# A first expert's tokens gathered apart from its group, and fewer warming matmuls ahead of the experts

## The chip, the cores and the metric

One core of a Trainium2 chip (trn2). The metric is device time in microseconds of one execution; the kernel before took 934.81 us (median of 3 runs, 934.11 to 937.46).

## The reference, cut to what matters

```python
for l in range(DEPTH):                       # DEPTH = 2
    h = rmsnorm(x, norm1_g[l]);  x = x + token_mixers(h, ...)      # four mixers, merged, projected
    h = rmsnorm(x, norm2_g[l]);  x = x + hierarchical_moe(h, ...)
return rmsnorm(x, norm_f_g)

def hierarchical_moe(h, ...):                # h: 256 tokens x 1024
    group = top1(softmax(h @ w_rg + b_rg))                         # 4 groups
    top2 experts of that group's 8, weights = p_group * softmax(their logits)
    # 32 experts, each: (silu(h @ w_g[e]) * (h @ w_u[e]) * comb[:, e]) @ w_d[e]
    # w_g[e], w_u[e]: 1024 x 256; w_d[e]: 256 x 1024, all float32
```

## The kernel before, in words

Each of the two layers is a mixer stage and an expert stage. The orders below are written out by hand, one program per engine, joined by semaphores (`then_inc`, `wait_ge`; `L(s, v)` is the value v counted within the layer).

**From mixer to experts.** VectorE adds the last projection to `x` (L1793, semaphore `x_mid`, once for each half of the tokens). TensorE transposes `x` (L711, 16 matmuls), multiplies it by the router's weights `wr` (L719, 16 matmuls whose moving operand is 36 columns wide), and then `keep_warm(11, 7)` issues 11 matmuls on constants whose result nobody reads (L403). Another `keep_warm(4, 7)` stands ahead of the transposes. VectorE meanwhile works out top-1 group and top-2 experts (L1813 to L1854, `member_ok`); TensorE ranks the tokens of each expert (L726 to L729), and VectorE makes `pick`, a 0/1 matrix of tokens by slots (L1861): a group of the kernel is GE = 4 experts, each has SLOTS = 32 slots, so that one group is 128 slots. There are 8 groups in a layer.

**A group's tokens.** `gather` (L740) multiplies `wide` (the normalised tokens, 128x128 blocks, as stationary operand) by `pick` (128 slots, as moving operand): 8 blocks of channels by 2 halves of the tokens, 16 matmuls in fp32, for which the profile shows 32 weight loads and 32 matmuls. Its two PSUM banks are scaled into `hG[g % 2]` by VectorE, 512 columns each (L1893, `gath_out`). `hG[0]` lies over `qkr`, `hG[1]` over `yy`.

**An expert.** `gate_up` (L753) multiplies the expert's 32 slots by its gate and up weights, 32 matmuls (64 in the profile), and signals `gu_mm`; ScalarE takes the SiLU (L1212), VectorE the product (L1904), TensorE transposes it (L759), `down` (L767) multiplies it by the down weights and signals `down_mm`. TensorE runs two experts ahead: `gate_up` of e + 2 stands before `down` of e. When e is a group's first expert, the gather of the next group stands before that.

**The weights.** SyncE's queue brings them, 1 MB a transfer, gate and up of an expert one behind the other (L340), down apart (L344). There is room for RP = 6 pairs and RD = 7 downs. `FIRST_LOADS` fills all of it; then every further transfer waits for its place:

```python
for kind, e in NEXT_LOADS:               # pairs 6, 7, 8, then pair 9, down 7, pair 10, down 8, ...
    if kind == "gu":
        sp.wait_ge(*L(gu_mm, e - RP + 1)); load_gate_up(sp, e, l)
    else:
        sp.wait_ge(*L(down_mm, e - RD + 1)); load_down(sp, e, l)
```

So pair 6 is asked for when `gate_up` of expert 0 is done, pair 7 after that of expert 1, pair 8 after that of expert 2. Behind the last expert's transfers the first units of the next layer's mixer weights follow on the same queue.

Of the kernel before, what the change touches and what calls it, by code (L numbers as in the profile page):

```python
# [17 lines left out]
P = 128  # L18
# [61 lines left out]
for _e in range(RD, NE):  # L80
# [16 lines left out]
    rank_mm=1, passes_ok=1,  # L97
    pick_ok=GROUPS, wpick_ok=GROUPS, gath_mm=2 * GROUPS, gath_out=2 * GROUPS, scat_T=GROUPS, scatT_out=GROUPS,
    gu_mm=NE, silu_out=NE, hid_out=NE, hid_T=NE, hidT_out=NE, down_mm=NE, y_act=NE, y_dve=NE,
# [3 lines left out]
def build(nc, x_in, positions, norm1_g, w_in, sgu_ln_g, sgu_ln_b, w_spatial, b_spatial, conv_w, w_branch,  # L103
          w_out, norm2_g, w_rg, b_rg, w_re, b_re, w_eg, w_eu, w_ed, norm_f_g, out):
    ctx = ExitStack()
    with ctx:
# [97 lines left out]
        def sem(name):  # L204
            return ctx.enter_context(nc.semaphore(name))
# [34 lines left out]
            sem("gexp"), sem("emax"), sem("eexp"), sem("member_ok"), sem("rank_mm"))  # L240
        passes_ok = sem("passes_ok")
        wide_mm = sem("wide_mm")
# [157 lines left out]
        def keep_warm(k, bank_no):  # L400

            for _ in range(k):
                nc.tensor.matmul(ps[:, bank_no, 0:P], ones[:], ident[:], start=True, stop=True,  # L403
                                 skip_group_check=True)
# [4 lines left out]
        def bank(b, n=1):  # L409
            return ps[:, b, :] if n == 1 else ps[:, b:b + n, :]  # L410


        with nc.Block() as whole:

            @whole.tensor
            def _(pe):
# [7 lines left out]
                for l in range(DEPTH):  # L424
# [281 lines left out]
                    pe.wait_ge(layer_loaded, 16 * 5 * (l + 1))  # L706
                    keep_warm(4, 7)
                    for t in range(TT):
# [6 lines left out]
                    for t in range(TT):  # L715
# [5 lines left out]
                        ins.then_inc(route_mm, 1)  # L721
                    keep_warm(11, 7)

# [9 lines left out]

                    def gather(g, dst_done):

                        for b in range(2):
                            for c in range(4):
                                cc = 4 * b + c
                                for t in range(TT):
                                    ins = mm(ps[:, b, P * c:P * c + P], wide[:, t, P * cc:P * cc + P],  # L740
                                             pick[:, t, :], start=(t == 0), stop=(t == TT - 1),
                                             skip_group_check=True)
                            if dst_done is gath_mm or b == 1:
                                ins.then_inc(dst_done, 1)
# [31 lines left out]
                    def gather_group(g):  # L776
                        pe.wait_ge(*L(pick_ok, g + 1))
                        if g == 0:
                            pe.wait_ge(*L(xn_act, 1))
                            pe.wait_ge(*L(xn_dve, 1))  # L780
                        if g >= 3:
                            pe.wait_ge(*L(x_add, 4 * (g - 2)))
                        gather(g, gath_mm)

                    def gate_up_expert(e):
                        pe.wait_ge(*gu_loads(e, l))
                        if e % GE == 0:
                            pe.wait_ge(*L(gath_out, 2 * (e // GE) + 1))
                        gate_up(pair_slot(e, l), hG[e // GE % 2], e % GE, 2 + e % 2, gu_mm,
                                L(gath_out, 2 * (e // GE) + 2) if e % GE == 0 else None)  # L790

# [24 lines left out]
                    def hid_expert(e):  # L816
# [3 lines left out]
                        hid_transposes(e % 2, hid_T)  # L820

                    gather_group(0)
                    gate_up_expert(0)
                    gate_up_expert(1)
# [624 lines left out]
            def _(dve):  # L1449
# [3 lines left out]
                def link(ins):  # L1453

                    n[0] += 1
                    ins.then_inc(dve_c, 1)
                    dve.wait_ge(dve_c, n[0])
# [37 lines left out]
                for l in range(DEPTH):  # L1495
# [388 lines left out]

                    link(V.tensor_reduce(cnts, ps[:, 2, 64:96], AX.X, ALU.max))
                    beyond = prod32.rearrange("p t g e -> p (t g e)")[:, 0:MAXPASS]
                    link(V.tensor_tensor(beyond, cnts.broadcast_to([P, MAXPASS]), limits[:], ALU.is_gt))
                    link(V.tensor_reduce(cnts, beyond, AX.X, ALU.add))
                    V.tensor_copy(npass[:], cnts[0:1, :]).then_inc(passes_ok, 1)

                    def gather_evac(dst, b):

                        return V.tensor_tensor(dst[:, 4 * b:4 * b + 4, :], bank(b).rearrange("p (c s) -> p c s", c=4),  # L1893
                                               small[:, PG2 + 4 * b:PG2 + 4 * b + 4]
                                               .rearrange("p (c o) -> p c o", o=1).broadcast_to([P, 4, P]), ALU.mult)

                    def gather_out(g):
                        for b in range(2):
                            dve.wait_ge(*L(gath_mm, 2 * g + b + 1))
                            gather_evac(hG[g % 2], b).then_inc(gath_out, 1)  # L1900

# [6 lines left out]
                    def hidden_expert(e):  # L1908
                        dve.wait_ge(*L(silu_out, e + 1))
                        hidden(e % 2, 2 + e % 2).then_inc(hid_out, 1)  # L1910

                    def add_group(g, banks):
                        for k in range(4):
# [3 lines left out]
                            V.tensor_tensor(xs, xs, bank(banks[k]), ALU.add).then_inc(x_add, 1)  # L1917

                    gather_out(0)
                    pick_group(1)  # L1920
                    hidden_expert(0)
                    hidden_expert(1)
# [83 lines left out]
```

## Time and profile before

| | |
|---|---|
| median of 3 runs | 934.81 us (934.11 to 937.46) |
| the profiled execution | 935.73 us, its span 934.0 us |
| TensorE busy / its weight loads | 843.5 us (90%) / 670.8 us (72%) |
| VectorE / ScalarE / GpSimd busy | 534.1 us (57%) / 389.5 us (42%) / 114.6 us (12%) |
| mean DMA rate | 301 GB/s; 281.45 MB moved |
| mean granted clock of TensorE | 0.958 of full speed |

Times in the rows are microseconds from the start of the span. PE is TensorE's matmuls, PEld its weight loads (they overlap), DVE VectorE, ACT ScalarE, POOL GpSimd, SPq SyncE's DMA issues. In brackets stands the idle time before a piece and what ended it. A busy TensorE says little by itself, since many of its matmuls are warming or wait on their weight loads; the order of events around one release says more.

### The profile page before, as it was taken

The page shows a single profiled execution, that of the slowest core. Times are in us where ns is not written, and L with a number is a line of the kernel's source. Part 1 is how long each engine was busy: PE and PEld are TensorE (multiplying, and loading weights), DVE is VectorE, ACT ScalarE, POOL GpSimd, SP SyncE. Part 2 cuts the span into 40 slices and gives each one's busy share as a digit, 9 for nine tenths or more (in the row PEclk, how much of TensorE's full clock was granted, in tenths as well). Part 3 has the DMA queues.
Part 4 walks back from the last instruction along what each step waited for, and adds up shares of the span by engine and source line. Part 5 has one row for each costly group of instructions (what it writes and reads, how often), then busy time and mean ns, then how long its engine had stood idle before and what let it go on. Part 6 is the DMA issues. An engine that isn't in the chain of part 4 may idle for free.

```text
span 934.0 us, 19930 instructions
## 1 busy us (share of the span) xinstructions
PE 843.5 (90%) x8583; PEld 670.8 (72%) x8583; DVE 534.1 (57%) x1072; ACT 389.5 (42%) x676; POOL 114.6 (12%) x168
## 2 busy tenths in 40 slices
PE   7999899999999988867899997999999999777775
PEld 6997778887987756654579976888789767554543
DVE  5677668667555533423476676885746555333424
ACT  5547667645412211111265567674544222211114
POOL 6700101211000000000055001022200000000000
PEclk9999999999999989988999999999999999988978
DMA  9965444473899999999996453456578999999993
GB/s 271 361 241 178 138 136 144 172 299 151 354 378 418 418 419 420 420 420 420 399 360 236 137 183 108 157 182 223 226 269 335 419 419 420 420 419 420 420 420 125
DMA packets 63516, 281.45 MB, mean 301 GB/s; under 512 B 5024, under 2 KB 7152, under 8 KB 38848
## 3 DMA queue, kind: packets, MB, share of 16 engines
q1 hardware_dynamic: 62144, 278.18, 76.6%
q0 software_dynamic: 800, 1.40, 0.9%
q8 instruction: 70, 1.15, 0.5%
q10 hardware_dynamic: 480, 0.54, 0.2%
q14 instruction: 22, 0.18, 0.1%
HBM read 279.06 MB, written 1.05 MB: 300 GB/s over the span
## 4 chain that ended last, share of the span: by engine, by line
PE 57%; DMA 18%; DVE 7%; ACT 7%; issue 5%; SPq 4%; POOL 2%; POOLq 0%; DVEq 0%; ACTq 0%
DMA ring<-in_w_exp_up 15%; PE ps L436 9%; PE ps L438 9%; PE ps L437 9%; PE ps L753 9%; PE ps L740 4%; PE ps L813 4%; PE ps L767 4%; DMA late<-in_w_exp_up 3%; SPq L340 3%; DVE split_lo L1506 2%; PE ps L403 2%; ACT split_hi L998 1%; POOL wide L1399 1%; PE ps L759 1%
## 5 line engine op out<-in xcount | busy, mean ns | idle before, releaser
L1506 DVE TENSOR_TENSOR split_lo<-ring,split_hi 128x1024 fp32r<-128x1024 f32 (+1 forms) x143 | 195.8, 1410 | 46.1 <-ACT split_hi L998 41.7
L436 PE MATMUL ps<-split_hi,hT_hi 128*128 128x512 f32 (+2 forms) x416 | 162.8, 391 | 15.7 <-DVE split_lo L1506 12.6
L438 PE MATMUL ps<-split_hi,hT_lo 128*128 128x512 f32 (+2 forms) x416 | 159.4, 383 | 0.0
L437 PE MATMUL ps<-split_lo,hT_hi 128*128 128x512 f32 (+2 forms) x416 | 159.4, 383 | 0.0
L998 ACT ACTIVATE split_hi<-ring 128x1024 fp32r<-128x1024 f32 (+1 forms) x140 | 141.4, 1053 | 27.3 <-PE ps L438 24.7
L1904 DVE TENSOR_TENSOR br<-br,ps 32x64 f32<-32x64 f32 x256 | 54.9, 214 | 162.9 <-ACT br L1212 160.3
L1212 ACT ACTIVATE br<-ps 128x64 f32<-128x64 f32 x64 | 14.3, 224 | 266.3 <-PE ps L753 266.3
L436 PEld LDWEIGHTS ps<-split_hi,hT_hi 128*128 128x128 f32 x416 | 79.4, 191 | 35.7 <-DVE split_lo L1506 17.8
L438 PEld LDWEIGHTS ps<-split_hi,hT_lo 128*128 128x128 f32 x416 | 79.3, 191 | 14.8
L437 PEld LDWEIGHTS ps<-split_lo,hT_hi 128*128 128x128 f32 x416 | 79.4, 191 | 13.4
L753 PE MATMUL ps<-ring,yy 128*32 128x128 f32 x1664 | 60.8, 306 | 24.2 <-DMA ring<-in_w_exp_up 24.1
L753 PEld LDWEIGHTS ps<-ring,yy 128*32 128x32 f32 x1664 | 52.1, 123 | 34.7 <-DMA ring<-in_w_exp_up 27.7
L753 PE MATMUL ps<-ring,qkr 128*32 128x128 f32 x1792 | 60.7, 293 | 17.9 <-DMA ring<-in_w_exp_up 17.2
L753 PEld LDWEIGHTS ps<-ring,qkr 128*32 128x32 f32 x1792 | 52.8, 118 | 25.6 <-DMA ring<-in_w_exp_up 22.8
L1416 POOL TENSOR_TENSOR idx<-idx,wt 128x128 f32<-128x128 f32 x32 | 12.1, 399 | 411.2 <-PE ps L773 327.6
L740 PEld LDWEIGHTS ps<-idx,wide 128*128 128x128 f32 x512 | 58.4, 192 | 5.0 <-issue 4.9
L740 PE MATMUL ps<-idx,wide 128*128 128x128 f32 x512 | 61.2, 278 | 0.0
L1399 POOL TENSOR_TENSOR wide<-wide,qkr 128x1024 f32<-128x1024 f32 x10 | 33.1, 3310 | 183.2 <-DVE qkr L1682 183.2
L1917 DVE TENSOR_TENSOR x<-x,ps 128x512 f32<-128x512 f32 x64 | 44.0, 688 | 16.0 <-PE ps L813 16.0
L767 PE MATMUL ps<-late,br 128*32 128x256 f32 x704 | 49.4, 399 | 1.3 <-DMA late<-in_w_exp_down 1.1
L436 PE MATMUL ps<-hT_hi,split_hi 128*128 128x256 f32 x160 | 45.6, 285 | 0.0
L437 PE MATMUL ps<-hT_lo,split_hi 128*128 128x256 f32 x160 | 45.3, 283 | 0.0
(264 smaller groups left out, 1274.9 us busy)
## 6 DMA issues: line engine op xcount, KB each, us to landing
ring<-in_w_exp_gate SPq DMA_DIRECT2D x54, 1024.0 KB, 24.6
ring<-in_w_exp_up SPq DMA_DIRECT2D x54, 1024.0 KB, 26.0
ring<-in_w_in SPq DMA_DIRECT2D x52, 1024.0 KB, 6.5
late<-in_w_exp_down SPq DMA_DIRECT2D x44, 1024.0 KB, 26.8
ring<-in_w_exp_down SPq DMA_DIRECT2D x20, 1024.0 KB, 26.7
late<-in_w_exp_gate SPq DMA_DIRECT2D x10, 1024.0 KB, 25.2
late<-in_w_exp_up SPq DMA_DIRECT2D x10, 1024.0 KB, 26.4
ring<-in_w_branch SPq DMA_DIRECT2D x8, 1024.0 KB, 4.9
```

Source lines behind the costliest of these rows:

```text
L436: mm(dst, st[0], mv[0], start=start, stop=False, skip_group_check=True)
L437: mm(dst, st[0], mv[1], start=False, stop=False, skip_group_check=True)
L438: return mm(dst, st[1], mv[0], start=False, stop=stop, skip_group_check=True)
L740: ins = mm(ps[:, b, P * c:P * c + P], wide[:, t, P * cc:P * cc + P], pick[:, t, :], start=(t == 0), stop=(t == TT - 1), skip_group_check=True)
L753: ins = mm(ps[32 * j:32 * j + 32, b, 0:P], hg[:, c, SLOTS * i:SLOTS * i + SLOTS], w[:, :, c, 64 * j:64 * j + 64], start=(c == 0), stop=(c ...
L767: ins = mm(ps[32 * q:32 * q + 32, b, 0:256], hidT[:, par, k, :], w[:, k, 256 * q:256 * q + 256], start=(k == 0), stop=(k == 1))
L813: mm(bank(banks[k]), scatT[:, t, :], y_slots[g % 2][:, 512 * hf:512 * hf + 512], start=True, stop=True).then_inc(scat_mm, 1)
L998: A(half_view(split_hi[:, v % SPLITS, :], v), raw_half(v, l), ACT.Copy).then_inc(hi_done, 1)
L1399: nc.gpsimd.tensor_tensor(m, m, sig[:], ALU.add).then_inc(gate_sum, 1)
L1506: V.tensor_tensor(half_view(split_lo[:, v % SPLITS, :], v), raw_half(v, l), half_view(split_hi[:, v % SPLITS, :], v).bitcast(F32), ALU.sub ...
L1904: ins = V.tensor_tensor(hid[:, par, 64 * j:64 * j + 64], silu[32 * j:32 * j + 32, par, :], ps[32 * j:32 * j + 32, b, 64:128], ALU.mult)
L1917: V.tensor_tensor(xs, xs, bank(banks[k]), ALU.add).then_inc(x_add, 1)
```

## The change

The first expert of group 0 gets a gather of its own. `gather_lead` runs the same 16 matmuls with only its 32 slots as moving operand, into PSUM bank 4; VectorE scales the result in one instruction of 256 columns, and `gate_up` of expert 0 waits for that (`lead_out`). The gather of group 0 follows behind it with the other 96 slots, its two evacuations 384 columns each, and `gate_up` of expert 1 waits for these. On VectorE the evacuation of the lead stands ahead of the last three steps of the pass count, for whose end GpSimd waits (`passes_ok`), and expert 0's product ahead of the gather's evacuations and of `pick` for group 1. `keep_warm(4, 7)` is gone and `keep_warm(11, 7)` is `keep_warm(8, 7)`. All of it holds for both layers.

```diff
-                    keep_warm(4, 7)
                     for t in range(TT):
                         pe.wait_ge(*L(x_mid, t + 1))
...
-                    keep_warm(11, 7)
+                    keep_warm(8, 7)
...
-                    def gather(g, dst_done):
+                    def gather(g, dst_done, s0=0):
...
-                                    ins = mm(ps[:, b, P * c:P * c + P], wide[:, t, P * cc:P * cc + P],
-                                             pick[:, t, :], start=(t == 0), stop=(t == TT - 1),
+                                    ins = mm(ps[:, b, P * c + s0:P * c + P], wide[:, t, P * cc:P * cc + P],
+                                             pick[:, t, s0:], start=(t == 0), stop=(t == TT - 1),
...
-                        gather(g, gath_mm)
+                        gather(g, gath_mm, SLOTS if g == 0 else 0)
+
+                    def gather_lead():
+                        pe.wait_ge(*L(pick_ok, 1))
+                        pe.wait_ge(*L(xn_act, 1))
+                        pe.wait_ge(*L(xn_dve, 1))
+                        for c in range(C):
+                            for t in range(TT):
+                                ins = mm(ps[:, 4, SLOTS * c:SLOTS * c + SLOTS], wide[:, t, P * c:P * c + P],
+                                         pick[:, t, 0:SLOTS], start=(t == 0), stop=(t == TT - 1), skip_group_check=True)
+                        ins.then_inc(lead_mm, 1)
...
                         pe.wait_ge(*gu_loads(e, l))
-                        if e % GE == 0:
+                        first_of = 1 if e < GE else 0
+                        if e == 0:
+                            pe.wait_ge(*L(lead_out, 1))
+                        elif e % GE == first_of:
                             pe.wait_ge(*L(gath_out, 2 * (e // GE) + 1))
...
+                    gather_lead()
+                    gate_up_expert(0)
                     gather_group(0)
-                    gate_up_expert(0)
                     gate_up_expert(1)
...
                     link(V.tensor_reduce(cnts, ps[:, 2, 64:96], AX.X, ALU.max))
+                    dve.wait_ge(*L(lead_mm, 1))
+                    V.tensor_tensor(hG[0][:, :, 0:SLOTS], ps[:, 4, 0:C * SLOTS].rearrange("p (c s) -> p c s", c=C),
+                                    small[:, PG2:PG2 + C].rearrange("p (c o) -> p c o", o=1).broadcast_to([P, C, SLOTS]),
+                                    ALU.mult).then_inc(lead_out, 1)
...
+                    hidden_expert(0)
                     gather_out(0)
                     pick_group(1)
-                    hidden_expert(0)
                     hidden_expert(1)
```

TensorE's order, layer 0, from the last projection (L438) to the gather of group 1 (L740, moving operand in columns behind the partitions; L753 is gate and up, 32 matmuls an expert). Before:

```order
L438 MATMUL ps<-split_hi,hT_lo 128x512
L403 MATMUL ps<-ident,ones 128x128 x4
L711 MATMUL ps<-ident,x 128x128 x16
L719 MATMUL ps<-wr,late 128x36 x16
L403 MATMUL ps<-ident,ones 128x128 x11
L726 MATMUL ps<-br,incl_T 128x64
L727 MATMUL ps<-br,ones 128x64
L729 MATMUL ps<-br,ones 128x32
L403 MATMUL ps<-ident,ones 128x128 x5
L740 MATMUL ps<-idx,wide 128x128 x16
L753 MATMUL ps<-ring,qkr 32x128 x64
L759 MATMUL ps<-ident,br 128x32 x2
```

The same place in the changed kernel (its lines are numbered a few lower or higher):

```order
L718 MATMUL ps<-wr,late 128x36 x16
L403 MATMUL ps<-ident,ones 128x128 x8
L725 MATMUL ps<-br,incl_T 128x64
L726 MATMUL ps<-br,ones 128x64
L728 MATMUL ps<-br,ones 128x32
L403 MATMUL ps<-ident,ones 128x128 x5
L787 MATMUL ps<-idx,wide 128x32 x16
L752 MATMUL ps<-ring,qkr 32x128 x32
L739 MATMUL ps<-idx,wide 128x96 x16
L752 MATMUL ps<-ring,qkr 32x128 x32
L758 MATMUL ps<-ident,br 128x32 x2
```

Sixteen matmuls on the same 16 blocks of `wide` are added ahead of expert 0, and the group's own gather, 96 columns wide, now stands between expert 0 and expert 1.

VectorE's order in the changed kernel, layer 0, from the expert weights `wt` on (L1897 is the lead's evacuation, L1907 the gather's, L1919 an expert's product, L1871 `pick`):

```order
L1891 TENSOR_TENSOR wt<-br 128x64
L1895 TENSOR_REDUCE br<-ps 128x1
L1897 TENSOR_TENSOR qkr<-ps,small_all 128x8x32
L1901 TENSOR_TENSOR br<-br,limits 128x8
L1902 TENSOR_REDUCE br<-br 128x1
L1903 CAST npass<-br 1x1
L1919 TENSOR_TENSOR br<-br,ps 32x64 x4
L1907 TENSOR_TENSOR qkr<-ps,small_all 128x4x96 x2
L1871 TENSOR_TENSOR idx<-rankm,slot_no 128x2x128
L1919 TENSOR_TENSOR br<-br,ps 32x64 x4
```

Before, the two evacuations of 512 columns and `pick` for group 1 stood right behind `npass`, ahead of both products.

## Rows read from the trace of the kernel before

**Rows 1.** The page: the DMA rate (GB/s) in 40 equal slices of the span.
```profile
GB/s 271 361 241 178 138 136 144 172 299 151 354 378 418 418 419 420 420 420 420 399 360 236 137 183 108 157 182 223 226 269 335 419 419 420 420 419 420 420 420 125
```

**Rows 2.** The chain that ended last, in order of time: start us, us, what.
```profile
446.36 3.50 PE ps L753 x64
...
875.74 26.32 DMA ring<-in_w_exp_up
902.11 3.64 PE ps L753 x64
```

**Rows 3.** Stretches around the first release of a pair in each layer; columns in the first line.
```profile
core 0: us, PE busy (x) PEld busy (x) DVE busy (x) ACT busy (x) POOL busy (x), PEclk, DMA share, GB/s
260.00:263.50 3.50, 3.50 (x96) 3.34 (x98) 1.26 (x3) 0.22 (x1) 0.00 (x0) 1.00 0.65 269
263.50:267.00 3.50, 3.50 (x71) 3.26 (x63) 1.71 (x8) 0.45 (x2) 0.00 (x0) 1.00 0.82 272
716.00:719.50 3.50, 3.50 (x111) 3.34 (x114) 1.51 (x5) 0.22 (x1) 0.00 (x0) 1.00 0.62 255
719.50:723.00 3.50, 3.07 (x52) 2.57 (x41) 1.23 (x6) 0.45 (x2) 0.00 (x0) 1.00 0.97 318
```

**Rows 4.** SyncE's DMA issues in order of time, layer 0: start us, us, line, transfer.
```profile
263.24 0.33 SPq L340 DMA_DIRECT2D ring<-in_w_exp_gate  x1
...
264.98 0.33 SPq L340 DMA_DIRECT2D ring<-in_w_exp_gate  x1
...
270.99 0.33 SPq L340 DMA_DIRECT2D ring<-in_w_exp_gate  x1
...
274.08 0.33 SPq L340 DMA_DIRECT2D ring<-in_w_exp_gate  x1
```

**Rows 5.** The same, layer 1.
```profile
718.72 0.33 SPq L340 DMA_DIRECT2D ring<-in_w_exp_gate  x1
...
721.13 0.33 SPq L340 DMA_DIRECT2D ring<-in_w_exp_gate  x1
...
727.16 0.33 SPq L340 DMA_DIRECT2D ring<-in_w_exp_gate  x1
```

**Rows 6.** Timeline, layer 0, from the last residual add to expert 1.
```profile
244.31 2.65 DVE L1793 TENSOR_TENSOR x<-x,ps 128x512 f32<-128x512 f32 x4 [7.20 <-PE ps L438]
...
246.25 1.78 PEld L711 LDWEIGHTS ps<-ident,x 128*128 128x128 f32 x16
...
248.00 3.66 PEld L719 LDWEIGHTS ps<-wr,late 128*128 128x128 f32 x32
...
251.57 4.17 PEld L403 LDWEIGHTS ps<-ident,ones 128*128 128x128 f32 x22
...
254.91 0.22 DVE L1854 TENSOR_TENSOR br<-br 128x64 f32<-128x64 f32 x1
255.66 0.30 PEld L726 LDWEIGHTS ps<-br,incl_T 128*128 128x128 f32 x2
...
257.45 3.65 PEld L740 LDWEIGHTS ps<-idx,wide 128*128 128x128 f32 x32
...
261.22 3.43 PEld L753 LDWEIGHTS ps<-ring,qkr 128*32 128x32 f32 x128
...
261.33 0.69 DVE L1893 TENSOR_TENSOR qkr<-ps,small_all 128x512 f32<-128x512 f32 x1 [1.09 <-PE ps L740]
261.94 0.42 DVE L1861 TENSOR_TENSOR idx<-rankm,slot_no 128x256 f32<-128x256 f32 x1
```

**Rows 7.** Timeline, layer 1, warming and the start of the ranking.
```profile
707.56 2.54 PEld L403 LDWEIGHTS ps<-ident,ones 128*128 128x128 f32 x22
...
710.87 0.22 DVE L1854 TENSOR_TENSOR br<-br 128x64 f32<-128x64 f32 x1
711.15 0.30 PEld L726 LDWEIGHTS ps<-br,incl_T 128*128 128x128 f32 x2 [1.05 <-DVE br L1854]
```

**Rows 8.** A stretch of layer 0 with the granted clock (PEclk), same columns as rows 3.
```profile
251.50:255.00 3.50, 3.50 (x19) 3.50 (x19) 2.78 (x19) 2.98 (x5) 0.00 (x0) 0.51 1.02 431
```

More of the change, by code:

```diff
@@ L97 @@
     rank_mm=1, passes_ok=1,
-    pick_ok=GROUPS, wpick_ok=GROUPS, gath_mm=2 * GROUPS, gath_out=2 * GROUPS, scat_T=GROUPS, scatT_out=GROUPS,
+    lead_mm=1, lead_out=1, pick_ok=GROUPS, wpick_ok=GROUPS, gath_mm=2 * GROUPS, gath_out=2 * GROUPS, scat_T=GROUPS, scatT_out=GROUPS,
     gu_mm=NE, silu_out=NE, hid_out=NE, hid_T=NE, hidT_out=NE, down_mm=NE, y_act=NE, y_dve=NE,
@@ L240, in build @@
             sem("gexp"), sem("emax"), sem("eexp"), sem("member_ok"), sem("rank_mm"))
-        passes_ok = sem("passes_ok")
+        passes_ok, lead_mm, lead_out = sem("passes_ok"), sem("lead_mm"), sem("lead_out")
         wide_mm = sem("wide_mm")
@@ L777, in gather_group @@
                         pe.wait_ge(*L(pick_ok, g + 1))
-                        if g == 0:
-                            pe.wait_ge(*L(xn_act, 1))
-                            pe.wait_ge(*L(xn_dve, 1))
                         if g >= 3:
                             pe.wait_ge(*L(x_add, 4 * (g - 2)))
-                        gather(g, gath_mm)
+                        gather(g, gath_mm, SLOTS if g == 0 else 0)
[8 more added lines that the diff above has]
+                        ins.then_inc(lead_mm, 1)
                     def gate_up_expert(e):
                         pe.wait_ge(*gu_loads(e, l))
-                        if e % GE == 0:
+                        first_of = 1 if e < GE else 0
+                        if e == 0:
+                            pe.wait_ge(*L(lead_out, 1))
+                        elif e % GE == first_of:
                             pe.wait_ge(*L(gath_out, 2 * (e // GE) + 1))
                         gate_up(pair_slot(e, l), hG[e // GE % 2], e % GE, 2 + e % 2, gu_mm,
-                                L(gath_out, 2 * (e // GE) + 2) if e % GE == 0 else None)
+                                L(gath_out, 2 * (e // GE) + 2) if e and e % GE == first_of else None)
                     def down_expert(e):
@@ L1889, in _, with gather_evac @@
                     V.tensor_copy(npass[:], cnts[0:1, :]).then_inc(passes_ok, 1)
-                    def gather_evac(dst, b):
-                        return V.tensor_tensor(dst[:, 4 * b:4 * b + 4, :], bank(b).rearrange("p (c s) -> p c s", c=4),
+                    def gather_evac(dst, b, s0=0):
+                        return V.tensor_tensor(dst[:, 4 * b:4 * b + 4, s0:],
+                                               bank(b).rearrange("p (c s) -> p c s", c=4)[:, :, s0:],
                                                small[:, PG2 + 4 * b:PG2 + 4 * b + 4]
-                                               .rearrange("p (c o) -> p c o", o=1).broadcast_to([P, 4, P]), ALU.mult)
+                                               .rearrange("p (c o) -> p c o", o=1).broadcast_to([P, 4, P - s0]), ALU.mult)
                     def gather_out(g):
@@ L1899, in gather_out @@
                             dve.wait_ge(*L(gath_mm, 2 * g + b + 1))
-                            gather_evac(hG[g % 2], b).then_inc(gath_out, 1)
+                            gather_evac(hG[g % 2], b, SLOTS if g == 0 else 0).then_inc(gath_out, 1)
                     def hidden(par, b):
```

## The prediction

> **What bounds the kernel now.** I read the DMA rate over the span first. In each expert stage it stands at 418 to 420 GB/s slice after slice [rows 1]: there the kernel takes weights as fast as they come. The chain that ended last confirms it: in both layers it ends on a weight transfer of over 26 us and then on the `gate_up` that had waited for it [rows 2]. So a microsecond in which the DMA engines stand idle early in an expert stage is missing at its end, and a microsecond that TensorE gains or loses there counts only if it moves a transfer. The question is then when the queue runs dry, and for that I read short stretches and SyncE's issues.
>
> `FIRST_LOADS` asks for all that there is room for, and the next issue is that of pair 6 at 263.24 [rows 4], when expert 0's `gate_up` has freed a place. In the 3.5 us up to 263.5 the mean rate is 269 GB/s and in the 3.5 us behind it 272 [rows 3]. Against the full 420 that is a flow that ends at 260 + 3.5 x 269/420 = 262.24 and one that begins at 267 - 3.5 x 272/420 = 264.73: 2.5 us idle, and 1.49 us from the issue to the flow. In layer 1 the same working gives 718.13 and 720.35 [rows 3], 2.2 us idle, and 1.63 us behind the issue at 718.72 [rows 5]. These two holes, 4.7 us together, are all that an earlier expert 0 could win.
>
> **The lead gather.** The group's gather takes 3.65 us of weight loads for 32 of them, and 3.77 us pass from its start at 257.45 to that of `gate_up` at 261.22 [rows 6]. What does a moving operand of 32 columns save? The router's matmuls have the same 128-column stationary operand and only 36 moving columns, and their 32 loads take 3.66 us [rows 6], the same. So the stationary side sets the pace and the narrower operand saves nothing: I take 3.77 us. The other bound is the `gate_up` form, whose 128 loads are 32 columns wide and take 3.43 us, 27 ns each [rows 6]: 32 x 27 ns = 0.9 us if the loads cost nothing at all. The router's row is by far the nearer, so the sum goes by it. TensorE: Matmul & The Clock Gate, a page of the Trainium skill, has in its section on the back-to-back issue gap a form by which the spacing is N/2.4 + 2.5 ns with a floor of about 25 ns, which would make the lead some 0.8 us (an estimate by that page); with that the sum would be the third rival's below. The trace disagrees here (3.66 us at 36 moving columns, 3.65 at 128).
>
> **What stands between it and expert 0.** Before, `gate_up` began as the gather ended, for the first half had been evacuated meanwhile, and the second evacuation (261.33, 0.69 us) was needed only at half way [rows 6]. Now TensorE must wait for the lead's evacuation: 0.11 us from the matmul's end to VectorE (261.22 to 261.33), 0.42 us for 256 columns (the `pick` of that size), 0.06 us back to TensorE (VectorE's last routing step ends at 710.87 + 0.22 = 711.09, and TensorE begins at 711.15 [rows 6, 7]). That is a bubble of 0.59 us. VectorE's chain of small steps is over long before; the three `npass` steps behind the wait delay GpSimd's first product by some 3 us, which nobody needs before the transposes two experts later: nothing.
>
> **Warming.** `keep_warm(4)` ends at 246.25, where the transposes begin; the residual adds end at 244.31 + 2.65 = 246.96 and the second half of the transposes needs them [rows 6], at 246.25 + 0.89 = 247.14 before and 247.02 now. Of the 1.0 us taken out, 0.12 us is won. `keep_warm(11)` ran until 255.66 in layer 0 though `member_ok` was there at 254.91 + 0.22 = 255.13 [rows 6], since the granted clock was 0.51, the 1.2 GHz level, in that stretch [rows 8]. With three matmuls fewer and 0.12 us won ahead of it, the ranking starts when `member_ok` comes, at 255.13 - 0.12 + 0.06 = 255.07, 0.59 us earlier. In layer 1 the warming was over early and TensorE waited 1.05 us for VectorE [rows 7]: only the 0.12 us there. Savings: 0.59 and 0.12 us.
>
> **Expert 0** then ends at +0.59 - 0.59 = 0 in layer 0 and at +0.59 - 0.12 = +0.47 us in layer 1. It is not earlier. **Experts 1 and 2** come a whole gather later, for the other 96 slots need all 16 stationary blocks once more: another 3.77 us. Their evacuations (each under 0.69 us) are hidden, the first under the gather's second half, the second under the first half of `gate_up` (3.7/4 = 0.9 us); expert 0's product, now ahead of them, is done before the first. So the releases of pairs 7 and 8 come 3.77 us later in layer 0 and 3.77 + 0.47 = 4.24 us later in layer 1.
>
> **What of it reaches the DMA queue.** A pair is 2.1 MB, 4.99 us at 420 GB/s; pair 8 would begin to flow two pairs behind the restart. Layer 0: before at 264.73 + 9.98 = 274.71; now its issue is at 270.99 + 3.77 = 274.76 [rows 4] and its flow 1.49 us later, 276.25: **1.5 us lost**. Pair 7's own lateness (268.75 + 1.49 against 269.72, half a microsecond) lies within that, since the latest release decides. Layer 1: before at 720.35 + 9.98 = 730.33; now 727.16 + 4.24 + 1.63 = 733.03 [rows 5]: **2.7 us lost**. Pair 9 is asked for 3.1 us behind pair 8 (270.99 and 274.08 [rows 4]), while pair 8's 5 us still flow, and what follows has more in hand. What of the 1.5 us from issue to flow still counts when the queue is not quite empty, no row shows; from below it is nothing, which gives 0.1 and 1.1 us, from above the whole of it, which gives 1.5 and 2.7. The queue would have only about half a microsecond left at those issues, so I take the upper value.
>
> **Sum:** +4.2 us. The profiled execution (935.73 us) is 0.9 us above the median of 934.81; against the median that makes **939.0 us**, 0.45% slower.
>
> **Rivals.** *The clock falls in the lead.* In layer 0 it fell to the 1.2 GHz level at 251.5, right behind the 3.66 us of narrow router matmuls, and came back at 255 [rows 6, 8]; in layer 1, same instructions, it did not. The lead gather is another narrow stretch of the same length with an idle bubble behind it. If the clock falls there, it is expert 0 and the second gather that run slowly: the same 22 warming loads took 4.17 us in layer 0 and 2.54 in layer 1, so 1.6 us a fall [rows 6, 7], all of it on the release of pair 8. In one layer that gives 940.6, in both 942.2. The same page of the Trainium skill says that the clock gate falls when TensorE is little used, and the trace bears it out once in two such places; so about one in three for each lead, a third of the chance altogether.
> *The latency from issue to flow is hidden* by what is left in the queue: +1.2 us, 936.0, to some 938 if half of it is.
> *Not slower: narrow matmuls are short after all.* With the lead at 0.9 us, expert 0 ends 2.9 and 2.4 us earlier, and both holes close. Pair 8 then decides: its release shifts by 3.77 - 2.87 + 0.59 less the savings, +0.9 and +1.37 us, its flow begins at 273.4 instead of 274.7 and at 730.2 instead of 730.3: -1.5 us, 933.3. If 96 columns are in proportion cheaper too (2.8 us), it is -3.4 us, 931.4. The two layers break even, by the same working, at a lead of some 1.6 us. Against it stands the router's row.
> *The change doesn't reach its place:* it would need a wait that holds the lead, but `pick` and the normalised tokens are both there when the gather starts today.
>
> **Chances.** Forecast 0.40, clock 0.33, hidden latency 0.15, not slower 0.06, something unseen 0.06 (either side). A measurement of this kernel can tell about 0.5% (4.7 us, so 930.1 to 939.5) from no change. The forecast lies just inside, with its own spread of half a microsecond a layer about two thirds of it; with the latency case, the not-slower case and a little of the clock case that makes 0.52 for no change, 0.46 for slower, 0.02 for faster. The range runs from the hidden latency, 936.0, to a fall in both layers, 942.3.
>
> **What would show it.** Right: in the changed kernel, 32 weight loads of 3.6 us for the lead and again for the 96 columns; TensorE idle 0.6 us between lead and expert 0; pair 6 issued no earlier behind the ranking than before, pairs 7 and 8 about 4 us later; a DMA hole ahead of pair 6 as before and a second one of a microsecond ahead of pair 8; everything from there to the end of the layer shifted by 1.5 to 2.7 us. Wrong: a lead well under 3 us, or a queue that never runs dry a second time.

## The result and the profile after

The changed kernel took 949.02 us (median of 4 runs, 944.12 to 950.75) against 934.66 us before: ratio 1.014, 95% interval 1.0119 to 1.0161. I had forecast 939.0 us in a range of 936.0 to 942.3. The sign is right and the size is not: 14.4 us are lost instead of 4.2. The profiled execution took 950.75 us, its span 948.8 us, 14.8 longer than before.

The page of the changed kernel, the DMA rate over 40 slices [rows 1]:

```profile
GB/s 271 364 226 175 133 134 176 136 347 128 379 317 422 418 420 420 420 420 420 395 350 205 146 180 91 152 191 232 204 252 284 377 419 419 420 419 420 420 421 143
```

The two expert stages still run at 418 to 422 GB/s once they run; it is the slices just ahead (317; 284 and 377) that got thin. The chain of the changed kernel still ends on weights and on the `gate_up` that waited for them [rows 2], so the loss was suffered where the queue was dry:

```profile
423.77 27.58 DMA ring<-in_w_exp_up
451.40 3.64 PE ps L752 x64
...
891.03 26.55 DMA ring<-in_w_exp_up
917.62 3.31 PE ps L752 x64
```

The timeline of the changed kernel around the lead in layer 0 (L787 is the lead, L752 `gate_up`, L739 the other 96 slots, L1897 the lead's evacuation), beside [rows 6]:

```profile
257.43 3.65 PEld L787 LDWEIGHTS ps<-idx,wide 128*128 128x128 f32 x32
...
261.30 0.42 DVE L1897 TENSOR_TENSOR qkr<-ps,small_all 128x256 f32<-128x256 f32 x1 [2.75 <-PE ps L787]
...
261.84 2.51 PEld L752 LDWEIGHTS ps<-ring,qkr 128*32 128x32 f32 x64 [0.76 <-issue]
...
264.74 4.27 PEld L739 LDWEIGHTS ps<-idx,wide 128*128 128x128 f32 x32 [0.38 <-issue]
...
269.11 1.69 PEld L752 LDWEIGHTS ps<-ring,qkr 128*32 128x32 f32 x64
```

The lead's 32 weight loads take 3.65 us with 32 moving columns, as those of the full gather did. TensorE then stands 0.76 us. But expert 0's loads take 2.51 us where expert 1's take 1.69, and the second gather's 4.27 where the lead's took 3.65: the granted clock had fallen. Layer 1, the same place:

```profile
719.27 1.54 PEld L403 LDWEIGHTS ps<-ident,ones 128*128 128x128 f32 x10
720.69 6.95 PEld L787 LDWEIGHTS ps<-idx,wide 128*128 128x128 f32 x32
728.42 3.22 PEld L752 LDWEIGHTS ps<-ring,qkr 128*32 128x32 f32 x64 [0.78 <-issue]
732.02 4.44 PEld L739 LDWEIGHTS ps<-idx,wide 128*128 128x128 f32 x32 [0.38 <-issue]
736.56 1.69 PEld L752 LDWEIGHTS ps<-ring,qkr 128*32 128x32 f32 x64
```

Here the lead itself took 6.95 us. The stretches of the changed kernel say why (columns as in [rows 3]: TensorE, its loads, VectorE, ScalarE, GpSimd, granted clock, DMA share, GB/s):

```profile
262.50:266.00 3.50, 3.50 (x57) 3.12 (x47) 0.85 (x4) 0.22 (x1) 0.57 (x2) 0.52 0.32 59
...
718.00:721.50 3.50, 2.89 (x20) 2.89 (x20) 2.28 (x13) 1.16 (x1) 0.00 (x0) 0.79 1.01 426
721.50:725.00 3.50, 3.50 (x18) 3.50 (x18) 0.01 (x1) 0.00 (x0) 0.00 (x0) 0.50 1.01 421
725.00:728.50 3.50, 2.82 (x18) 2.72 (x21) 0.58 (x3) 0.00 (x0) 0.00 (x0) 0.50 0.22 87
728.50:732.00 3.50, 3.50 (x64) 3.14 (x64) 0.21 (x2) 0.00 (x0) 0.76 (x2) 0.50 0.00 0
732.00:735.50 3.50, 3.50 (x28) 3.48 (x25) 1.42 (x5) 0.23 (x1) 0.00 (x0) 0.76 0.66 227
```

In layer 0 the clock is at the 1.2 GHz level from 262.7 to 266.1. In layer 1 it stays there from 720.1 to 733.7, 13.7 us, through the end of the warming, the lead, its bubble, expert 0 and the start of the second gather, with TensorE all but continuously busy. The DMA engines, which had been drained by 725.7, stand still until 733.6: eight microseconds where there had been two. SyncE's issues in layer 1 [rows 5]:

```profile
732.14 0.33 SPq L340 DMA_DIRECT2D ring<-in_w_exp_gate  x1
...
738.57 0.33 SPq L340 DMA_DIRECT2D ring<-in_w_exp_gate  x1
...
744.58 0.33 SPq L340 DMA_DIRECT2D ring<-in_w_exp_gate  x1
```

Counted from the issue of pair 5 at the mixer's end (701.65 before, 709.28 after), pairs 6, 7 and 8 are asked for at 22.9, 29.3 and 35.3 us instead of 17.1, 19.5 and 25.5.

**A measure for all runs.** For every profile I took the times of these issues from pair 5's on, and the DMA rate in 60 stretches of 1 us, from 4 us behind pair 5's issue on, summed as (420 - rate)/420: the DMA time that is missing in that part. The table stands behind the experiments.

### The profile page after: what moved, and what is told of

The parts are those of the page before. It is cut to its first block, busy times and chain, and to the rows that moved or that the text cites. A ratio compares the mean times of both kernels' runs of the same rounds, so it can differ in the third digit from the quotient of the medians.

```text
span 948.8 us, 20010 instructions
## 1 busy us (share of the span) xinstructions
PE 861.0 (91%) x8619; PEld 682.9 (72%) x8619; DVE 533.8 (56%) x1074; ACT 389.6 (41%) x676; POOL 114.5 (12%) x168
## 3 DMA queue, kind: packets, MB, share of 16 engines
HBM read 279.06 MB, written 1.05 MB: 295 GB/s over the span
## 4 chain that ended last, share of the span: by engine, by line
PE 59%; DMA 18%; DVE 7%; ACT 7%; issue 5%; SPq 2%; POOL 2%; DVEq 0%; POOLq 0%; ACTq 0%
DMA ring<-in_w_exp_up 14%; PE ps L436 10%; PE ps L752 9%; PE ps L438 9%; PE ps L437 9%; PE ps L739 5%; PE ps L766 4%; PE ps L822 4%; DMA late<-in_w_exp_up 3%; DVE split_lo L1516 2%; PE ps L403 2%; ACT split_hi L1008 1%; SPq L340 1%; POOL wide L1409 1%; PE ps L758 1%
## 5 line engine op out<-in xcount | busy, mean ns | idle before, releaser
L436 PE MATMUL ps<-split_hi,hT_hi 128*128 128x512 f32 (+2 forms) x416 | 162.9, 392 | 16.9 <-DVE split_lo L1516 13.7
L438 PE MATMUL ps<-split_hi,hT_lo 128*128 128x512 f32 (+2 forms) x416 | 159.4, 383 | 0.0
L1008 ACT ACTIVATE split_hi<-ring 128x1024 fp32r<-128x1024 f32 (+1 forms) x140 | 141.5, 1053 | 27.1 <-PE ps L438 25.3
L1919 DVE TENSOR_TENSOR br<-br,ps 32x64 f32<-32x64 f32 x256 | 54.9, 215 | 161.9 <-ACT br L1222 159.3
L438 PEld LDWEIGHTS ps<-split_hi,hT_lo 128*128 128x128 f32 x416 | 79.5, 191 | 14.8
L752 PE MATMUL ps<-ring,yy 128*32 128x128 f32 x1664 | 61.5, 309 | 24.5 <-DMA ring<-in_w_exp_up 24.5
L752 PEld LDWEIGHTS ps<-ring,yy 128*32 128x32 f32 x1664 | 52.6, 124 | 35.0 <-DMA ring<-in_w_exp_up 27.8
L752 PE MATMUL ps<-ring,qkr 128*32 128x128 f32 x1792 | 62.7, 298 | 13.1 <-DMA ring<-in_w_exp_up 11.7
L752 PEld LDWEIGHTS ps<-ring,qkr 128*32 128x32 f32 x1792 | 54.1, 119 | 21.2 <-DMA ring<-in_w_exp_up 16.0
L739 PEld LDWEIGHTS ps<-idx,wide 128*128 128x128 f32 x512 | 59.9, 196 | 6.3 <-issue 6.2
L739 PE MATMUL ps<-idx,wide 128*128 128x128 f32 (+1 forms) x512 | 63.1, 282 | 0.1
```

Of the source, the lines that this page charges most:

```text
L436: mm(dst, st[0], mv[0], start=start, stop=False, skip_group_check=True)
L438: return mm(dst, st[1], mv[0], start=False, stop=stop, skip_group_check=True)
L739: ins = mm(ps[:, b, P * c + s0:P * c + P], wide[:, t, P * cc:P * cc + P], pick[:, t, s0:], start=(t == 0), stop=(t == TT - 1), skip_group_ ...
L752: ins = mm(ps[32 * j:32 * j + 32, b, 0:P], hg[:, c, SLOTS * i:SLOTS * i + SLOTS], w[:, :, c, 64 * j:64 * j + 64], start=(c == 0), stop=(c ...
L1008: A(half_view(split_hi[:, v % SPLITS, :], v), raw_half(v, l), ACT.Copy).then_inc(hi_done, 1)
L1919: ins = V.tensor_tensor(hid[:, par, 64 * j:64 * j + 64], silu[32 * j:32 * j + 32, par, :], ps[32 * j:32 * j + 32, b, 64:128], ALU.mult)
```

## The experiments

Theory A, from the trace: the narrow lead drops the clock. Rival B: the missing warming does. Rival C: the clock hardly matters, and the extra gather costs the DMA queue much more than the 4.2 us that I worked out. The first four kernels cross the two parts: lead narrow or wide, warming cut or whole.

**e1, the changed kernel with both warming blocks back.**

```diff
+                    keep_warm(4, 7)
                     for t in range(TT):
...
-                    keep_warm(8, 7)
+                    keep_warm(11, 7)
```

> The changed kernel with both warming blocks as before (4 and 11 matmuls). Theory A (the narrow lead gather itself, 3.65 us of 32-column matmuls and a 0.6 us bubble, drops the granted clock in expert 0 and the second gather): the clock still falls there in most executions, 943 to 947 us. Rival B (the missing warming drops the clock): no fall in the lead, 939 to 940 us. Rival C (neither: the extra gather costs far more at the DMA queue than the 4.2 us I gave it): 947 to 950 us, with the clock full.

Measured: 941.99 us (936.68 to 945.52, 7 runs) against 934.36, ratio 1.0089 (1.0056 to 1.0122). In its profile the clock fell right behind the lead, in expert 0, in layer 0 (260.1 to 263.5), and not in layer 1. The median lies between A's range and B's, nearer to A's, and the clock still fell with all the warming back: B falls as the whole cause. Yet the warming is worth 5.5 to 6.7 us here: the kernel is 7.6 us slower than the one before, and the change 14.4 (13.1 when it was measured again, e10 below).

**e2, the kernel before with the cut warming and no lead.**

```diff
-                    keep_warm(4, 7)
...
-                    keep_warm(11, 7)
+                    keep_warm(8, 7)
```

> The kernel before with the two cuts in warming alone (no block of 4, 8 instead of 11), no lead gather. A: nothing to lose, ranking up to 0.6 us earlier, 934.0 to 934.8 us. B: the clock falls in the gather or in expert 0, 937 us or more. C: as A.

Measured: 936.71 us (934.13 to 938.16, 10 runs), ratio 1.0018 (1.0002 to 1.0034). What I had counted as a gain of 0.7 us is a loss of 1.7 us (0.2 to 3.2). The weight loads of its layer 1 show a part of it:

```profile
709.33 1.87 PEld L403 LDWEIGHTS ps<-ident,ones 128*128 128x128 f32 x16
712.91 0.30 PEld L725 LDWEIGHTS ps<-br,incl_T 128*128 128x128 f32 x2 [1.71 <-DVE br L1853]
...
713.58 2.10 PEld L403 LDWEIGHTS ps<-ident,ones 128*128 128x128 f32 x10
715.55 4.42 PEld L739 LDWEIGHTS ps<-idx,wide 128*128 128x128 f32 x32
```

TensorE idles 1.71 us behind the shorter warming, the clock falls at 713.7 and the full gather takes 4.42 us instead of 3.65. In the kernel before, the clock fell in layer 0 only, during the warming itself [rows 6, 8], where it cost half a microsecond. In layer 0 of e2 it did not fall here at all, and pair 8 is asked for 0.7 us earlier: there the saving came. So only a part of the loss is traced. The two layers together miss 0.6 us more DMA time than before; of the 2.4 us by which this profile's span is longer, 1.6 lie in the mixer of layer 1, which the edit does not touch.

**e3, the changed kernel with a wide lead.** Same order, waits and number of loads, but all 128 slots as moving operand, written into banks 0 and 1 instead of bank 4.

```diff
-                                ins = mm(ps[:, 4, SLOTS * c:SLOTS * c + SLOTS], wide[:, t, P * c:P * c + P],
-                                         pick[:, t, 0:SLOTS], start=(t == 0), stop=(t == TT - 1), skip_group_check=True)
+                                ins = mm(ps[:, c // 4, P * (c % 4):P * (c % 4) + P], wide[:, t, P * c:P * c + P],
+                                         pick[:, t, :], start=(t == 0), stop=(t == TT - 1), skip_group_check=True)
...
-                    V.tensor_tensor(hG[0][:, :, 0:SLOTS], ps[:, 4, 0:C * SLOTS].rearrange("p (c s) -> p c s", c=C),
+                    V.tensor_tensor(hG[0][:, :, 0:SLOTS], ps[:, 0:2, :].rearrange("p b (c s) -> p (b c) s", c=4)[:, :, 0:SLOTS],
```

> The changed kernel, but the lead gather takes all 128 slots as moving operand (into banks 0 and 1, of which only expert 0's 32 slots are evacuated): same 32 weight loads, same order, same waits, wide matmuls. A: the clock stays full through lead, expert 0 and second gather, 938.5 to 940 us; pairs 7 and 8 asked for 3.8 and 4.2 us later than before. B: as the changed kernel, 944 to 950 us. C: 947 to 950 us with the clock full.

Measured: 942.20 us (940.67 to 943.33, 4 runs), ratio 1.0086 (1.0064 to 1.0107). Four times as many moving columns in the lead make the kernel 5.3 to 6.5 us faster. C falls, and B as the whole cause. A's 940 us at most is missed by 2: the clock did not stay full, it fell behind the short warming, as B has it, and the lead's loads took 4.89 us. But it came back within the lead, and expert 0 and the second gather ran at full speed:

```profile
254.01 1.63 PEld L403 LDWEIGHTS ps<-ident,ones 128*128 128x128 f32 x10
255.52 4.89 PEld L787 LDWEIGHTS ps<-idx,wide 128*128 128x128 f32 x32
261.25 1.72 PEld L752 LDWEIGHTS ps<-ring,qkr 128*32 128x32 f32 x64 [0.84 <-issue]
263.17 3.65 PEld L739 LDWEIGHTS ps<-idx,wide 128*128 128x128 f32 x32 [0.20 <-issue]
```

**e4, the wide lead and both warming blocks** (the edits of e1 and e3 together).

> The wide lead and both warming blocks as before. A: 939.0 to 940.5 us (the bubble of 0.6 us without the 0.6 and 0.1 us saved). B: the same, since warming is there. C: 947 us or more.

Measured: 940.59 us (939.19 to 943.07, 4 runs), ratio 1.0072 (1.0045 to 1.0099). A holds. This is what the change costs when the clock falls neither in the lead nor behind it: its profile has falls in the warming alone, and 3.65 us of loads for the lead in both layers. The rest of the steps, in layer 1:

```profile
718.13 3.65 PEld L788 LDWEIGHTS ps<-idx,wide 128*128 128x128 f32 x32
722.63 1.72 PEld L753 LDWEIGHTS ps<-ring,qkr 128*32 128x32 f32 x64 [0.84 <-issue]
724.54 3.65 PEld L740 LDWEIGHTS ps<-idx,wide 128*128 128x128 f32 x32 [0.20 <-issue]
728.28 1.69 PEld L753 LDWEIGHTS ps<-ring,qkr 128*32 128x32 f32 x64
```

**e5, the second gather's time alone.** Sixteen wide matmuls on constants in the kernel before:

```diff
                     gate_up_expert(0)
+                    keep_warm(16, 7)
                     gate_up_expert(1)
```

> The kernel before with 16 wide matmuls on constants between expert 0 and expert 1: the second gather's TensorE time alone, no lead, no bubble, no cut in warming. If the loss of the wide lead with full warming (940.6 us against 934.4) is the later release of pairs 7 and 8, this gives releases of pairs 7 and 8 3.8 us later and a DMA hole ahead of pair 8 in each layer: +1.5 and +2.2 us, 937.5 to 938.5 us. If the bubble and the evacuation ahead of expert 0 are the larger part, 935 to 936 us. If something else of the change (order on VectorE, GpSimd's later start) carries it, 934.4 us.

Measured: 939.08 us (935.91 to 941.64, 10 runs) against 935.32, ratio 1.0034 (1.0016 to 1.0052), which is 3.2 us (1.5 to 4.9), and 3.8 by the medians. The first case holds. In layer 0 the filler takes the gather's 3.65 us and the issues follow it:

```profile
263.32 0.33 SPq L340 DMA_DIRECT2D ring<-in_w_exp_gate  x1
...
268.98 0.33 SPq L340 DMA_DIRECT2D ring<-in_w_exp_gate  x1
...
274.98 0.33 SPq L340 DMA_DIRECT2D ring<-in_w_exp_gate  x1
```

Pair 6 stands where it stood [rows 4], pairs 7 and 8 come 3.9 us later from pair 5's issue on.

**e6, the changed kernel with the 11 back, the 4 still out.**

```diff
-                    keep_warm(8, 7)
+                    keep_warm(11, 7)
```

> The changed kernel with 11 warming matmuls instead of 8; the block of 4 ahead of the transposes stays out. If the three matmuls taken from behind the router are what lets the clock fall into the narrow lead, this is as the changed kernel with both blocks back, 941 to 943 us. If the block of 4 does it, about 947 to 949 us. Both in equal parts: 944 to 946 us.

Measured: 943.40 us (936.06 to 949.49, 10 runs), ratio 1.0066 (1.0039 to 1.0094). Mostly the first case: the three matmuls behind the router carry most of what warming does here. The runs lie in groups, two at 936.1, seven from 941.5 to 944.1, one at 949.5. In its profile (943.36 us) the clock fell in both layers, in expert 0 for 3 us in layer 0, and in the lead for 7 us in layer 1.

**e7, another way at the same DMA hole.** The kernel before, but half a place given back in the middle of expert 0:

```diff
+                            if first and c == C // 2 - 1:
+                                ins.then_inc(gu_half, 1)
...
+                        if kind == "gu" and e == RP:
+                            sp.wait_ge(*L(gu_half, 1))
+                            load_half_pair(sp, e, l, 0)
+                            sp.wait_ge(*L(gu_mm, 1))
+                            load_half_pair(sp, e, l, 1)
```

> The kernel before, with the place of pair 0 given back in two halves: after the first four of eight channel blocks of expert 0's gate and up, SyncE asks for the first halves of pair 6's gate and up (0.5 MB each), after the last block for the second halves. It goes at the same DMA hole as the change, without a gather more. First issue 0.9 us earlier, DMA hole 0.9 us shorter in each layer: 932.5 us against 934.4, ratio 0.998. If halves of 0.5 MB flow slower or the hole is not what sets the end: 934.4 or more.

Measured: 936.16 us (933.73 to 941.46, 12 runs), ratio 1.0005 (0.9988 to 1.0023): no gain. The issue did come 0.9 us earlier (16.7 us behind pair 5's instead of 17.6), and then the stretches of layer 0 show a slow flow (first e7, then the kernel before, whose issue is at 263.24):

```profile
263.00:264.00 1.00, 1.00 (x48) 1.00 (x41) 0.00 (x0) 0.12 (x1) 0.00 (x0) 1.00 0.22 49
264.00:265.00 1.00, 1.00 (x48) 1.00 (x40) 0.82 (x4) 0.11 (x1) 0.00 (x0) 1.00 0.82 229
265.00:266.00 1.00, 1.00 (x26) 0.76 (x16) 0.15 (x2) 0.27 (x2) 0.00 (x0) 1.00 0.80 320
266.00:267.00 1.00, 1.00 (x10) 1.00 (x11) 0.74 (x4) 0.18 (x1) 0.00 (x0) 1.00 1.03 209
267.00:268.00 1.00, 1.00 (x12) 1.00 (x11) 0.06 (x1) 0.00 (x0) 0.00 (x0) 1.00 0.62 184
268.00:269.00 1.00, 1.00 (x12) 1.00 (x11) 0.63 (x1) 0.00 (x0) 0.00 (x0) 1.00 0.94 242
...
265.00:266.00 1.00, 1.00 (x9) 0.96 (x10) 0.71 (x4) 0.44 (x2) 0.00 (x0) 1.00 0.89 377
266.00:267.00 1.00, 1.00 (x12) 1.00 (x11) 0.14 (x1) 0.00 (x0) 0.00 (x0) 1.00 1.01 426
```

Behind the restart in the kernel before the rate is above 420 GB/s within three microseconds of the issue; with halves, of 4 KB to a partition instead of 8, it stays at 184 to 320 for five, and the missing DMA time is 3.6 and 2.5 us instead of 2.3 and 2.1. Whether the size of the pieces or the four issues close together are to blame was not tried.

**e8, the bubble filled.** The changed kernel with two wide warming matmuls where TensorE waits for the lead's evacuation:

```diff
                         ins.then_inc(lead_mm, 1)
+                        keep_warm(2, 7)
```

> The changed kernel with two wide warming matmuls (0.5 us) in the bubble between the narrow lead and expert 0, where TensorE waits anyway. If the bubble is what the clock falls on, 942 to 944 us, as with the wide lead; if it is the narrow gather and the thinner warming ahead of it, as the changed kernel beside it, 946 to 950 us.

Measured: 949.36 us (945.39 to 950.22, 4 runs), ratio 1.0144 (1.0101 to 1.0187). It is not the bubble that makes the kernel so slow. In its profile the clock was down for 13.7 us in both layers; in layer 0 for most of that time:

```profile
254.00:267.50 13.50, 13.50 (x112) 12.66 (x110) 2.62 (x14) 0.22 (x1) 0.76 (x2) 0.50 0.46 191
```

TensorE is busy in all 13.5 us of this stretch. The clock had fallen at 253.9, before the lead began at 255.3, and at 718.1 in layer 1, so this run doesn't show whether the bubble has a part where the clock falls behind the lead.

**e9, most of the second gather left out.** The kernel of e4, with 4 of the second gather's 16 matmuls (channel blocks 3 and 7). The wide lead has already written all 128 slots of both banks, so in the other blocks experts 1 to 3 of group 0 find the lead's own result.

```diff
                                 cc = 4 * b + c
+                                if s0 and c < 3:
+                                    continue
```

> The wide lead with full warming (940.6 us), its second gather cut from 16 matmuls to 4 (channel blocks 3 and 7 alone; experts 1 to 3 of group 0 compute with what is left of the lead in the other blocks). What stays is the lead's bubble ahead of expert 0. If bubble and second gather add up with the filler's 3.2 us, the bubble is worth 0.6 us a layer: 935.5 to 937 us. If splitting in itself costs more than the second gather's time, 938 us or more. If expert 0 did come earlier by being split off: 934 or less.

Measured: 937.48 us (935.44 to 943.24, 10 runs), ratio 1.0049 (1.0025 to 1.0073). That is 2.9 us over its own before by the medians and 4.6 (2.3 to 6.8) by the ratio: between the first case and the second, and the run doesn't decide between them. It is not faster: splitting expert 0 off gains nothing even with the second gather nearly gone. Pair 6 is asked for 0.7 us later than before in both layers, as the bubble says. Pairs 7 and 8 come 2.9 us later in layer 0: the bubble, 1.1 us of matmuls, and another 1.0 us in which TensorE stands until the first of the two evacuations is done. What this run also shows: with a wide lead the second gather computes nothing new. A kernel without any of it was not tried.

**e10, the changed kernel again.**

> The changed kernel once more, beside the two others on the same chip: 944 to 951 us, in groups as the clock falls in the leads of one or both layers and stays down for one or several microseconds; a profile in which it does not fall in a lead would be 939 to 941 us.

Measured: 947.73 us (946.49 to 955.70, 4 runs), ratio 1.0165 (1.0109 to 1.0222). That is 13.1 us over its own before by the medians. In its profile the clock was down for 13.7 us in layer 0 and for 3.4 us, in expert 0, in layer 1: the first measurement's pattern, with the layers exchanged.

**The table.** Issues of pairs 6, 7 and 8 in us from pair 5's issue, and the missing DMA time, from one profiled execution each:

| kernel | layer 0: pairs 6, 7, 8 | DMA missing | layer 1: pairs 6, 7, 8 | DMA missing |
|---|---|---|---|---|
| before | 17.6, 19.3, 25.3 | 2.3 | 17.1, 19.5, 25.5 | 2.1 |
| e5, filler | 17.6, 23.2, 29.2 | 4.0 | 17.6, 23.2, 29.2 | 4.1 |
| e9, second gather cut | 18.3, 22.2, 28.2 | 4.0 | 17.8, 21.7, 27.7 | 3.5 |
| e2, warming cut alone | 16.9, 18.6, 24.6 | 1.7 | 18.5, 20.3, 26.3 | 3.3 |
| e4, wide lead, full warming | 18.3, 23.9, 29.9 | 4.8 | 18.3, 23.9, 29.9 | 4.9 |
| e3, wide lead | 19.3, 24.9, 30.9 | 5.6 | 19.3, 24.9, 30.9 | 5.8 |
| e1, full warming | 19.4, 25.5, 31.5 | 6.6 | 17.7, 23.4, 29.4 | 4.3 |
| e6, block of 4 out | 19.5, 25.3, 31.3 | 6.0 | 19.8, 26.0, 32.0 | 7.1 |
| the change | 18.7, 25.0, 31.0 | 5.7 | 22.9, 29.3, 35.3 | 10.1 |
| e10, the change again | 23.0, 29.3, 35.3 | 10.0 | 18.7, 24.8, 30.8 | 5.8 |
| e8, bubble filled | 23.5, 29.4, 35.4 | 10.3 | 23.3, 29.4, 35.4 | 10.4 |

**Where the clock fell.** Read in the same profiles and e7's, the falls to the 1.2 GHz level sort by what TensorE did ahead of them and behind them.

- Eight warming matmuls left TensorE idle for 1.7 us ahead of the ranking in eight stretches (e2, e3 and e8 in both layers, the change in layer 1, e10 in layer 0). In seven of them the clock fell within 1.5 us behind that; in layer 0 of e2 it did not. With eleven matmuls and 1.05 us idle (layer 1 of the kernel before, e1, e6, e7, e9) it did so in none of five; in e6 it fell later, in the lead, for 6.8 us.
- Of these seven falls, the three with 128 moving columns behind them (e2, e3 twice) lasted 3.4 us, and the four with the narrow lead behind them (the change, e10, e8 twice) 13.7 us.
- Where the first fall lay in the warming, it cost little. The clock then fell a second time, in expert 0 and for 3.4 us, in all four cases with a narrow lead (the change and e10 in their other layer, e1 and e6 in layer 0), and in none of the seven with a wide lead or the full gather (layer 0 of the kernel before, e7 and e9; both layers of e4 and e5).

## Why the prediction was wrong

The step that failed is the clock. The sum took it as full in the lead, in expert 0 and in the second gather, and so did the savings by less warming. By the medians the change costs 6.2 us where it is full there (e4) and 14.4 as it was made (13.1 in e10).

**What bounds the kernel: right.** The last chain still ends on weights, and the missing DMA time follows the release of pair 8 by the prediction's own arithmetic. For e4: in layer 0 the issue at 29.9 us and 1.49 us to the flow, against 29.0 us before (264.73 + 9.98 - 245.67), is 2.4 us; measured 4.8 - 2.3 = 2.5. For the change in layer 1: 35.3 + 1.63 - 28.7 = 8.2; measured 8.0. The upper bound was the right one of the two for the latency, so the rival of a hidden latency falls. The same arithmetic comes within 0.3 us of the missing time in both layers of every row of the table but e9's. There it gives 0.7 us in each layer, and 1.7 and 1.4 are missing; why was not tried.

**The lead gather costs as much as the full one: right.** It takes 3.65 us of loads at 32 moving columns where the clock is full. The rival of short narrow matmuls falls. The section of TensorE: Matmul & The Clock Gate, in the Trainium skill, from which the prediction took its 0.8 us gives that form for a matmul by itself, and says that at few columns it comes out too low for matmuls that each have a weight load. These have one each, so the trace contradicts the use that I made of the form, and not the section.

**The bubble: right.** From the lead's first load to expert 0's I had 3.77 + 0.59 = 4.36 us; it was 4.41 behind a narrow lead (257.43 to 261.84) and 4.50 behind a wide one (e4). The 0.76 and 0.84 us for which the loads stand hold 0.12 us that the 3.77 already count.

**Expert 0 is not earlier, experts 1 and 2 come a gather later: right.** With the clock full, expert 0's release comes 0.7 us later in layer 0 than before (e4), and pair 8's 4.6 and 4.4 us later, where 3.77 + 0.59 without any saving would be 4.36. The filler alone costs 3.8 us by the medians and +1.7 and +2.0 us of missing DMA time; the whole with the clock full, e4, 6.2 us by the medians and +2.5 and +2.8.

**The savings by less warming: wrong, the first step that failed.** "Savings: 0.59 and 0.12 us" took the clock as given. In layer 0 of e2, where the clock stayed full, the saving came, 0.7 us on pair 8; in layer 1 a fall came into ranking and gather, and pair 8 was asked for 0.8 us later. Alone the cut costs 1.7 us (0.2 to 3.2, the interval of e2's ratio), of which the missing DMA time shows 0.6. I had looked at what the warming delays and not at what it prevents.

**The rival of the clock: right in mechanism, wrong in chance and in one size, and it decides the result.** I gave it "about one in three for each lead" and "1.6 us a fall". Of the six leads in three profiles of narrow lead and cut warming (the change twice, e8), all six had the clock down in the lead or in expert 0; with the 11 matmuls back it was three of four (e1, e6); of the six wide leads (e3, e4, e9) none had it down for expert 0. A fall of 3.4 us costs what I said: pair 8 at 31.0 and 30.8 us against 29.4 in e1's layer 1, where none fell. But in four of those six the clock stayed down for 13.7 us, and pair 8 was asked for at 35.3 to 35.4, 6.0 us late. The prediction had no such case: it took the length of the one fall it could see [rows 8], which ended in wide matmuls, for the length of any.

**The sum.** By the medians, the split with a wide lead and full warming costs 6.2 us (e4). The narrow lead adds 1.4 to that (e1, 7.6) and the cut in warming 1.6 (e3, 7.8), neither of them clear of the noise; both together add 8.2 (the change, 14.4; 6.9 by e10), which is. Of the profiled execution's 14.8 us of span, the missing DMA time is 3.3 + 8.0 = 11.3. 1.6 us lies in the mixer of layer 1, where a clock fall took another place than before; the same runs to and fro between executions of the kernel before, which range over 6 us. The remaining 1.9 us, half a microsecond of it ahead of the first expert stage, I have not traced.

## What to carry to other kernels

In a stage that lives on prefetched weights, write down when each place is given back and when the queue runs dry; an edit to the compute side is worth what it does to the latest of these releases, and that sum came out within 0.3 us here in all but one kernel. Splitting a matmul by its moving columns halves nothing when the stationary loads set its pace, and the same loads must be paid again for the rest. Before warming matmuls are cut, look for the next stretch with few moving columns and ask what is on the path if the clock falls there: warming has to be judged together with the narrow work behind it, not by the idle time it fills.

## What the runs showed of the hardware

TensorE's granted clock stayed at its lower level, 1.2 GHz, for 13.7 us in e8, and in the 13.5 us of the stretch shown TensorE's matmuls were busy without a gap, the narrow lead and expert 0 most of them; it was back within 2 us of the start of the 96-column gather. With 128 moving columns in the lead (e3) it was back before the lead was over, after 3.4 us. TensorE: Matmul & The Clock Gate, a page of the Trainium skill, tells in its part on the clock gate of a clock that rises once TensorE has been busy for a while. By the busy time that a profile shows, this trace does not agree. That the clock falls when TensorE is little used, which the prediction takes from the same page, fits the seven falls behind 1.7 us of idleness. It doesn't fit the fall of [rows 8], ahead of which the profile shows TensorE busy without a gap from 244 to 251.5 us.

A DMA queue restarted with 0.5 MB pieces ran at 184 to 320 GB/s for five microseconds (e7, layer 0), while behind a restart with 1 MB pieces the rate was at 377 and then 426 in the second and third (the kernel before).
